# First mixer with memory and short causal steps in turn, other PSUM banks, and idle products at four norms

## The reference

```
layer 0: h = rmsnorm(x); mixer_a: latent attention of 8 heads over 128 keys
         that an indexer picks for each query (score = sum over 16 heads of
         relu(q_idx . k_idx) * w_idx, top 128 of the causal ones)
layer 1: mixer_b: 16 heads, band of 128 keys, sink logits
both:    memory attention of 4 heads over 256 memory rows; w_out; residual;
         rmsnorm; gated feed-forward of width 2816 with a 3-tap convolution
second block: adaptive norms; mixer_c: 8 heads over a band and 256 context
         rows, beside a Fourier mix; gates, merge, w_out; norm; feed-forward
```

## Time and profile before

| what | value |
|---|---|
| median of 3 runs | 2065.3 us (2063.54 to 2065.39) |
| profiled execution, its own time | 2068.74 us |
| its span | 2066.8 us |
| PE busy | 2008.0 us |
| DVE busy | 1076.8 us |
| ACT busy | 711.1 us |
| POOL busy | 842.9 us |
| mean granted clock of TensorE | 0.986 |

### The profile page before, as it was taken

One profiled execution on the slowest core, in us unless ns is written; L12 is line 12 of the kernel. 1 busy time (PEld: TensorE's weight loads), 2 busy tenths in 40 slices (PEclk: granted clock), 3 DMA queues, 4 the chain that ended last, 5 costly groups with the idle time before them and its releaser, 6 DMA issues.

```text
span 2066.8 us, 26302 instructions
## 1 busy us (share of the span) xinstructions
PE 2008.0 (97%) x9871; PEld 1620.8 (78%) x9871; DVE 1076.8 (52%) x1980; ACT 711.1 (34%) x1288; POOL 842.9 (41%) x642
## 2 busy tenths in 40 slices
PE   9998899999999999999999999999999999999998
PEld 7776568788888885568888888888777878888887
DVE  7687754545644667745443544463233575312434
ACT  5234562322222236643222223434444433212222
POOL 4335015454554541124554554443222543444543
PEclk9999899999999999999999999999999999999999
DMA  5212003423523520014225323322111221222222
GB/s 208 77 66 105 4 14 104 163 93 114 199 93 123 224 91 34 27 39 146 103 81 194 124 99 104 121 85 79 42 44 46 95 102 62 102 90 98 87 97 77
DMA packets 31636, 199.24 MB, mean 96 GB/s; under 512 B 3632, under 2 KB 3760, under 8 KB 12720
## 3 DMA queue, kind: packets, MB, share of 16 engines
q1 hardware_dynamic: 27072, 167.22, 22.9%
q10 hardware_dynamic: 4464, 30.67, 3.9%
HBM read 195.78 MB, written 2.10 MB: 96 GB/s over the span
## 4 chain that ended last, share of the span: by engine, by line
PE 52%; issue 1%; DVE 1%; POOL 1%; ACT 1%; ACTq 0%; DVEq 0%; POOLq 0%
PE psum L1819 38%; PE psum L2427 6%; PE psum L1841 3%; PE psum L2018 1%; PE psum L1983 1%; POOL w_lo L644 1%; PE psum L2000 1%; PE psum L2322 1%; POOL w_lo_third L644 0%; PE psum L2375 0%; PE psum L1946 0%; PE psum L2057 0%; PE psum L2310 0%; DVE work L1427 0%; PE psum L2368 0%
## 5 line engine op out<-in xcount | busy, mean ns | idle before, releaser
L644 POOL TENSOR_TENSOR w_lo<-raw,w_hi 128x512 fp32r<-128x512 f32 (+2 forms) x624 | 828.6, 1357 | 1165.1 <-ACT w_hi L676 1165.1
L1819 PE MATMUL psum<-h_hi,w_hi 128*128 128x512 f32 x1496 | 593.2, 396 | 5.5 <-DVE f_lo L1664 2.6
L1819 PE MATMUL psum<-h_hi,w_lo 128*128 128x512 f32 x1496 | 583.7, 390 | 0.0
L1819 PE MATMUL psum<-h_lo,w_hi 128*128 128x512 f32 x1496 | 583.3, 390 | 0.0
L676 ACT ACTIVATE w_hi<-raw 128x1024 fp32r<-128x1024 f32 (+1 forms) x342 | 312.1, 961 | 449.1 <-PE psum L1819 355.5
L1819 PEld LDWEIGHTS psum<-h_hi,w_hi 128*128 128x128 f32 x1496 | 280.9, 188 | 79.6 <-issue 17.8
L1819 PEld LDWEIGHTS psum<-h_hi,w_lo 128*128 128x128 f32 x1496 | 281.1, 188 | 59.8
L1819 PEld LDWEIGHTS psum<-h_lo,w_hi 128*128 128x128 f32 x1496 | 281.3, 188 | 55.6
L810 ACT ACTIVATE work<-work 128x512 f32<-128x512 f32 x66 | 41.7, 632 | 388.4 <-DVE work L1427 388.4
L1423 DVE TENSOR_SCALAR work<-psum,params 128x512 f32<-128x512 f32 x66 | 53.4, 810 | 173.6 <-PE psum L1819 167.0
L1819 PE MATMUL psum<-g_hi,w_hi 128*128 128x512 f32 x352 | 137.4, 390 | 0.7 <-POOL w_lo L644 0.7
(11 more groups left out here) (416 smaller groups left out, 2867.3 us busy)
## 6 DMA issues: line engine op xcount, KB each, us to landing
raw<-w_up SPq DMA_DIRECT2D x66, 1024.0 KB, 4.8
mod_w<-w_mod ACTq DMA_DIRECT2D x24, 1024.0 KB, 6.2
raw<-w_dn SPq DMA_DIRECT2D x32, 704.0 KB, 4.1
raw<-w_c_in SPq DMA_DIRECT2D x13, 1024.0 KB, 4.8
raw<-w_dn SPq DMA_DIRECT2D x8, 1024.0 KB, 4.8
raw<-w_b_in SPq DMA_DIRECT2D x7, 1024.0 KB, 4.8
raw<-w_a_idx SPq DMA_DIRECT2D x5, 1024.0 KB, 6.0
raw<-w_a_out SPq DMA_DIRECT2D x8, 640.0 KB, 3.8
```

The costliest lines, as they stand in the source:

```text
L644: ins = nc.gpsimd.tensor_tensor(lo[:, a:z], RAW[slot][:, a:z], hi[:, a:z].bitcast(F32), ALU.subtract)
L1819: ins = nc.tensor.matmul(out, l, r, start=(k == 0 and m == 0), stop=(k == n - 1 and m == 2))
```

## The change

It has these parts:

1. The 8 memory steps and the 8 causal steps of query tile 0 alternate. Memory steps write to bank 7 and causal ones to bank 5, and a group of four waits for the flush of the group before the last. One rank tile (6 matmuls) goes into each of the first 13 steps, after 3 tiles ahead of the first step; `uk` and `uv` tiles are mixed (`RANK`). ACT copies one tile a step, and three ahead of its first step. DVE does two rounds of picking in steps 0 and 1 and one in each of the steps 2 to 13.
2. At place 18 of the index loop the dots come ahead of the wait and of the spread.
3. In the second mixer, three rounded pieces are split in halves over two steps.
4. `C_BANKS` ends with 1, 0, 1, 0.
5. `ffn1` gets 4 idle products between sums and spread, and `pre1` gets 5 ahead of its context products.
6. At `post1`, the terms go to PSUM banks 4, 5 and 6, and DVE multiplies before it copies. PE takes the first sums inside the last tile, behind 18 of its 24 matmuls. Eight idle products follow the last tile where three did, and three follow the second sums.

```diff
-        PART = [at(f"y_parts{i}", R + 24 + 4 * i, [2, S]) for i in range(2)]
+        PART = at("y_parts", R + 24, [2, S])
...
-        am_range = add_steps(mem_steps(0), ROWT, [whole(8), whole(9)])
-        a_range = add_steps(
...
+        for n, (memory, first_tile) in enumerate(zip(mem_steps(0), causal)):
+            for kind, s in enumerate((memory, first_tile)):
+                group = 2 * (n // 4) + kind
+                s.update(flush=group, freed=max(group - 1, 0), out_bank=7 - 2 * kind, first=n % 4 == 0, last=n % 4 == 3)
+                steps.append(s)
+        flushes.extend([whole(8), heads_of_tile(0, 0), whole(9), heads_of_tile(0, 1)])
+        a_range = add_steps(causal[A_HEADS:], 4, [heads_of_tile(t, h4) for t in range(1, ROWT) for h4 in range(2)])
...
+        MIXED = 2 * A_HEADS
+        RANK = [*(("uk", h) for h in range(3)), ("uv", 0), *(("uk", h) for h in range(3, 6)), ("uv", 1), ("uk", 6), ("uk", 7),
+                *(("uv", n) for n in range(2, 8))]
+        RANK_FIRST = 3
...
-        C_BANKS = [0, 1] * C_PAIRS + [1] * 8 + [0, 1] * 2
+        C_BANKS = [0, 1] * C_PAIRS + [1] * 8 + [1, 0] * 2
... ACT
             def a_between(k):
-                if k < 8:
-                    rank_copy(2 * k)
-                    rank_copy(2 * k + 1)
+                if k + RANK_FIRST < len(RANK):
+                    rank_copy(k + RANK_FIRST)
...
+            for i in range(RANK_FIRST):
+                rank_copy(i)
             attend(a_all, a_between)
...
             def b_between(k):
+                if begun:
+                    hi_split(begun.pop(), (1,))
...
                     if tile % 2 and tile < 6:
-                        hi_split(ph.split + 5 + tile // 2)
+                        hi_split(ph.split + 5 + tile // 2, (0,))
+                        begun.append(ph.split + 5 + tile // 2)
...
-                    if c > 2:
-                        act.wait_ge(y_added, c - 2)
+                    if 2 <= c < DC - 1:
+                        act.wait_ge(y_added, c - 1)
...
-                        dst = RUN[:, 2 * kind, :] if c == 0 else PART[c % 2][:, kind, :]
+                        dst = RUN[:, 2 * kind, :] if c == 0 else PART[:, kind, :] if c == DC - 1 else bank(5 + kind)
... DVE
             def a_between(k):
-                if k < 8:
+                if k < 2:
                     pick_eight(ROWT - 1, False)
-                    pick_eight(ROWT - 1, k == 7)
+                if k < MIXED - 2:
+                    pick_eight(ROWT - 1, k == MIXED - 3)
...
+                    step(nc.vector.scalar_tensor_tensor(out=RUN[:, 1, :] if m == 0 else bank(4), in0=y, scalar=DER[:, 2, m:m + 1],
+                                                        in1=XT[:, m, :], op0=ALU.mult, op1=ALU.mult))
+                    nc.vector.tensor_copy(Y[:, m, :], y).then_inc(ph.free, 1)
...
+                    step(nc.vector.tensor_tensor(RUN[:, 1, :], bank(4), RUN[:, 1, :], ALU.add))
                     v.wait_ge(y_parts, 2 * m + 1)
-                    step(nc.vector.tensor_tensor(RUN[:, 0, :], RUN[:, 0, :], PART[m % 2][:, 0, :], ALU.add))
+                    step(nc.vector.tensor_tensor(RUN[:, 0, :], bank(5), RUN[:, 0, :], ALU.add))
... PE
-                    elif name == "mix1":
-                        keep_busy(PH["b_in"], 4)
+                    elif name in ("mix1", "ffn1"):
+                        keep_busy(PH["b_in" if name == "mix1" else "up10"], 4)
...
+                dots(p)
                 if p == 18:
                     pe.wait_ge(x0_inverse, 2)
...
-                dots(p)
...
             def a_between(k, first):
-                if first and k < 7:
-                    advance(rank, FILL_MEM)
...
+                if k + RANK_FIRST < len(RANK):
+                    advance(rank, 6)
+                if k + 2 < MIXED and k % 2:
+                    pe.wait_ge(qkv_ready, 2 + (k + 1) // 2)
+                if k == 2:
+                    pe.wait_ge(PH["uv"].free, 1)
+                if k == 9:
+                    pe.wait_ge(PH["uv"].free, 2)
+                if k == MIXED:
...
             def first_rows():
+                bank_free(3)
+                for _ in range(5):
+                    nc.tensor.matmul(bank(3), CTXH[:, 0, 0:P], CTXH[:, 0:2, :], start=True, stop=True)
...
+            def run_sums(tile):
+                advance(tile, 18)
+                pe.wait_ge(y_added, DC - 2)
+                bank_free(4)
+                for kind in range(3):
+                    for t in range(ROWT):
+                        n = kind * ROWT + t
+                        ins = nc.tensor.matmul(bank(4, n, n + 1), RUN[:, kind, t * P:(t + 1) * P], ONES[:, 0:1], start=True, stop=True)
+                ins.then_inc(square_used, 1)
...
+            gemm(PH["c_out"], DC, 256, MH, ML, ready=lambda k: (m_lo, k + 1), between=lambda u: None, inside=run_sums)
             post1, pre2 = NORMS["post1"], NORMS["pre2"]
-            keep_busy(PH["up20"], 3)
-            pe.wait_ge(y_added, DC - 2)
+            keep_busy(PH["up20"], 8)
...
             ins.then_inc(square_used, 1)
+            keep_busy(PH["up20"], 3)
             pe.wait_ge(inverse_ready, SPREAD.index("post1") + 1)
```

More of the change, by code:

```diff
@@ L413, in add_steps @@
             for n, s in enumerate(group):
-                s["flush"] = len(flushes) + n // last_of
+                s["flush"] = s["freed"] = len(flushes) + n // last_of
+                s["out_bank"] = 7
                 s["first"] = n % last_of == 0
@@ L438, in mem_steps @@
                     for c in range(2) for t in range(ROWT)]
-        am_range = add_steps(mem_steps(0), ROWT, [whole(8), whole(9)])
-        a_range = add_steps(
[L442 to L446, removed]
+        causal = [
+            dict(nh=1, nk=(t + 1) * P, mask=cst("le", P) if t == 0 else PICK[:, t - 1, 0:(t + 1) * P],
+                 sink=None,
+                 qk=[(0, AQ[:, h, t * P:(t + 1) * P], AK[:, h, 0:(t + 1) * P])],
+                 pv=[[AV[:, kb_, h * P:(h + 1) * P] for kb_ in range(t + 1)]], out=[(0, P, h % 4)])
+            for t in range(ROWT) for h in range(A_HEADS)]
+        for n, (memory, first_tile) in enumerate(zip(mem_steps(0), causal)):
[5 more added lines that the diff above has]
+        a_range = add_steps(causal[A_HEADS:], 4, [heads_of_tile(t, h4) for t in range(1, ROWT) for h4 in range(2)])
         b_range = add_steps(
@@ L784, in flush @@
                     out = flushes[f][0]
-                    src = bank(7) if len(out.shape) == 2 else bank(7).rearrange("p (h n) -> p h n", h=4)
+                    src = bank(steps[s]["out_bank"])
+                    src = src if len(out.shape) == 2 else src.rearrange("p (h n) -> p h n", h=4)
                     nc.scalar.activation(out, src, ACT.Copy).then_inc(o_hi_ready, 1)
@@ L899, in _, with rank_copy @@
             uk, uv = PH["uk"], PH["uv"]
-            def rank_copy(n):
-                if n < 8:
+            def rank_copy(i):
+                name, n = RANK[i]
+                if name == "uk":
                     act.wait_ge(uk.done, n + 1)
-                    nc.scalar.activation(AK[:, n, :], bank(n % 2), ACT.Copy, scale=-(128 ** -0.5)).then_inc(uk.free, 1)
+                    nc.scalar.activation(AK[:, n, :], bank(i % 2), ACT.Copy, scale=-(128 ** -0.5)).then_inc(uk.free, 1)
                     act.wait_ge(uk.free, n + 1)
@@ L1844, in side_by_side, with gemm @@
                             yield
-            def gemm(ph, kc, width, act_hi, act_lo, rows=S, ready=None, first8=None, between=None):
+            def gemm(ph, kc, width, act_hi, act_lo, rows=S, ready=None, first8=None, between=None, inside=None):
                 t = ph.tiles
@@ L1871, in body @@
                             pe.wait_ge(ph.free, u * t + (c + 1 - period))
-                        advance(products(bank(b, 0, rows), [
+                        tile = products(bank(b, 0, rows), [
                             (HI[slot][:, k * width + c * P:k * width + (c + 1) * P],
@@ L1877, in body @@
                              ready(k) if ready is not None and isinstance(u, int) and u == 0 and c == 0 else None)
-                            for k in range(kc)], ph.done))
+                            for k in range(kc)], ph.done)
+                        if inside is not None and u == ph.n - 1 and c == t - 1:
+                            inside(tile)
+                        advance(tile)
                 if between is None:
@@ L2005, in values @@
                     st = steps[s]
-                    f = st["flush"]
                     pe.wait_ge(turned_ready, s + 1)
                     if st["first"]:
-                        if s > lo:
-                            pe.wait_ge(o_ready, f)
-                        else:
+                        if s == lo:
                             bank_free(7)
+                        elif st["freed"]:
+                            pe.wait_ge(o_ready, st["freed"])
                     kb_n = st["nk"] // P
@@ L2152, in rank_rest @@
             def rank_rest():
```

(14 more changed lines are left out.)

54 lines of the change are left out of this document (16 added, 38 removed).

## The result

The changed kernel takes 2049.58 us (median of 4 runs, 2048.22 to 2052.89) against 2065.35 (2063.54 to 2068.07): 15.8 us less, ratio 0.9926 with a 95% interval of 0.9911 to 0.9941. Forecast were 2043.0 and a range of 2034 to 2055. The profiled execution took 2048.22, 20.5 less than that of before (2068.74), where the forecast had 22.3 less. So the two profiles moved nearly as forecast and the medians by 5 us less. Two things are to be learnt here: why the two differ, and that the near match of the profiles is in part luck, since terms that missed in both directions cancel in it.

What follows compares the result with a forecast made beforehand. The order of PE's work was taken as the bound, with gains only in 58.8 us idle and in half-clock stretches. Terms summed to 22.3 us off the profiled 2068.74, giving 2046.4, or 2043.0 after 3.4 to the median; range 2034 to 2055.

Steps and rivals of the forecast that it cites:

- First mixer: Mixed steps, 202.80 us up to step 15's transposes: DVE's work is the limit; -9.0 us, between -12.5 and -3.
- One sign: First mixer: the clock would be 1.00 from 205 to 260 us if the forecast was right.
- Place 18: Index loop: the moved dots fall into a 2.4 us wait for the inverse; -1.05 us, between -1.1 and 0.
- C_BANKS: Fourier part, last four tiles: the 2.6 us wait on f_lo goes; -2.6 us, between -2.6 and 0.
- Halved pieces: Second mixer: halving ACT's rounding removes half the delay (3.2) and half clock (1.5); -4.7 us, between -7.5 and 0.
- The sign: Second mixer: three waits of PE under 1.4 us and none new, if the forecast was right.
- The norms: ffn1, mix1, ffn0: idle products delay slightly and may keep the clock; net -0.6 us, give or take 2.5.
- the sign that I had set: Norm term: wrong if a half-clock stretch appears at ffn0, or stays at pre1 and post1.
- pre1: At pre1: five idle products fill the 0.99 us gap before 13.66 us at half clock; -3.6 us, 5.5 at most.
- post1: At post1: sums inside the last tile, faster adds and idle products in waits; -0.8 us, from -2.8 to +2.
- Rival 1: Clock falls at norms by where in time they stand; pre1, norms, post1 give nothing: -14.8, 2050.5 us, chance 0.22.
- Rivals 2 and 3: First mixer: DVE's chain holds, 3.35 us a step, 2049.0, chance 0.12; memory chain counts each step, 4.3, 2072, chance 0.04.

Runs made afterwards that it cites:

- few_rounds: The changed kernel without the picking rounds of steps 2, 4, 6, 8, 10 and 12 (6 of 16 left out): 2045.62 us, ratio 0.9911.
- pre1_no_idle: The changed kernel without the five idle products at pre1: 2054.43 us, ratio 0.9958 to the kernel before.
- mix_alone: The kernel before with part 1 of the change alone, the other five parts undone: 2061.21 us, ratio 0.9969.
- post1_old: The changed kernel with part 6 undone, so post1 as before: 2052.56 us, ratio 0.9925.
- fine_pool: The changed kernel with POOL's w_lo of four pieces in instructions of 256 columns in place of 512: 2040.26 us, ratio 0.9876.

## Why the prediction was right, and where it was not

**First mixer.** Right in place and cause. Forecast -9.0, measured -9.9; the transposes of step 15 came at 247.77 where I had written 249. From DVE's first maximum to these transposes it is 46.3 us instead of 56.6. DVE is busy for 41.1 of them; my sum for its work was 43.6, with 4.0 for waits and clock on top. This is DVE's first maximum in the changed kernel:

```profile
201.43 0.76 DVE L1278 TENSOR_REDUCE stats<-psum 128x1 f32<-128x256 f32 x2
```

DVE is the limit, as forecast, but by few_rounds PE is some 2 us behind it, not 3.6. One sign did not come true: the clock was to be 1.00 from 205 on, and it is 0.50 for 3.41 us at 210.48. That cost little: pre1_no_idle, without this stretch, gains 10.2 in the section.

**Place 18 and C_BANKS.** -1.25 and -2.7 against -1.05 and -2.6: the wait for the inverse fell from 2.4 to 1.3, the one on `f_lo` went, and nothing took their place.

**Halved pieces.** The step that failed: "It takes away half of the delay, so 3.2". The delay was not ACT's. I had DVE's 2.39 us before me and called the wait "in part DVE's own". By the Trainium skill, "SBUF — State Buffer", section "Who interferes with whom", the shared port is held for a whole instruction and issue order decides who blocks. The trace agrees: two scalings took 0.62, 1.26 and 2.67 us beside no instruction of POOL, those of 256 columns and those of 512. I had weighed that rule against this very term (near 0, sum 4.7 worse), and did not make it a rival with a chance. Measured were +0.6 in place of -4.7, so the term missed by 5.3. The sign failed as well: the three waits were to come under 1.4 us, and in the changed kernel they are 2.92, 2.91 and 1.07, against 2.62, 2.62 and 1.08 before.

**The norms.** I wrote that mix1 fell for 6.82 us with its four idle products. That was a misreading: the stretch at 960.31 is at ffn1, which had none; mix1's was 3.41 us at 731.61. My 44.4 us at half clock also left out this stretch and two more of 3.41, at 205.96 and 902.28. The conclusion that idle products don't decide at ffn0, mix1 and ffn1 is not refuted all the same. mix1, whose code did not change, cost 1.6 us more in some traces and nothing in others, and ffn1 gained 1.5 in mix_alone without the idle products and 0.6 to 1.1 with them. Net +1.4 in the profile: in the bounds of -0.6 give or take 2.5, but the other way. By the sign that I had set the term is wrong, since a stretch at half clock appeared at ffn0 (353.84) and stayed at post1 (1657.73, 1664.56).

**pre1.** -3.6 forecast, -6.3 measured, beyond the 5.5 that I had called the most. The mis-sized term is the rest of the stretch: I let the other products wait for POOL or the root, but all of 13.66 us at half clock went. Sums and everything up to 1330.57 ran at 1.00.

**post1.** -0.9 in the profile, -0.8 forecast; the adds take 0.69 and the wait ahead of the first sums is gone, as forecast. The match of the two numbers is luck: the same code gives from -1.2 to +0.8 in eleven traces, and post1_old gives -0.6 without part 6.

**The sum of the profiles.** 22.3 forecast and 20.5 measured look closer than they are. Halved pieces gave 5.3 less than forecast and the norms 2.0 less. pre1 gave 2.7 more, the first mixer 0.9 more, and 1.6 came from the stretch at 902.28, of which no term speaks. That these nearly cancel is luck.

**From the profile to the median.** This is the other large mistake. I carried the 3.4 us between the profiled execution and the median to the result, as if they were in both. But the profiled execution of the changed kernel was the fastest of its four, 1.4 below its median. So the miss of 6.6 us between 2043.0 and 2049.58 is 1.8 from the profiles, 3.4 carried wrongly, and these 1.4. Over the experiments the kernel before ran 39 times. 26 of these lie between 2062.5 and 2065.8 us at a mean clock of 0.987 to 0.989, 13 between 2067.1 and 2072.5 at 0.984 to 0.986. The profiled execution (2068.74, 0.986) is among the upper ones. So it had more half clock than the usual execution, and I took 6.5 us of gains from its stretches (3.6 + 1.5 + 0.6 + 0.8). It is likely that a part of these gains could not show in the medians; that is argued from the clocks of the runs, as there is one profile of the kernel before.

Rival 1 (norms by where they stand) was 1 us from the median with 2050.5, nearer than my 2043.0, but in good part by luck: pre1's idle products do gain, and its 3.2 for the halves did not come. I had also written that pre1's fall starts exactly at its gap; the gap ends at 1334.15 and the fall is at 1335.77, 1.6 us later. Rivals 2 and 3 fell with the 46.3 us for 16 steps, where they had 53.6 and 68.8.

## What to carry to other kernels

Before a wait is put down to the engine that starts late, compare the duration of the same instruction with and without the neighbour: a scaling of 0.62 us that takes 2.67 names POOL, and dividing POOL's instructions gave 9 us where dividing ACT's gave none. An edit can be worthless until another limit is gone (halves gave nothing by themselves, and 2 to 3 us more than whole pieces once POOL's instructions were short). And a gain read from half-clock stretches of one profile is to be counted by how usual that profile is: look at the clock of all runs first, of the kernel before and of the changed one.

## What the runs showed of the hardware that was not expected

A DVE instruction of 128 x 2 elements took 1.24 us instead of 0.15 beside POOL's subtractions of 128 x 512, so even a very small one can wait for one of them, 1.26 us long. Not every kind does: in fine_pool a reciprocal of 128 x 2 took 0.17 us at 814.41, in the middle of POOL's row of seven from 813.55 on, and in the changed kernel the maximum with mask (line 1280), which reads PSUM, took 0.29 at 816.04 beside POOL's pair. Executions of one kernel spread over 10 us, ordered by the mean granted clock. They can be read as two groups (26 and 13 of 39, above) with means 6 us apart, but the gap between them, from 2065.82 to 2067.15, is little wider than the widest inside the upper one, 1.0 us. The Trainium skill, "TensorE: Matmul & The Clock Gate", section "Part 1: The HAM clock gate", says that the observation of activity doesn't restart with a kernel; two profiles of the changed kernel, one with a stretch at half clock at 28.18 us and one without, agree. That the spread of the times comes from it is argued, not shown.
